# Gate rows spread by products of depth one, and a later weight low part, in a fused two-block transformer kernel

## The reference

```python
mod_x = silu(c) @ w_mod + b_mod                      # 6 vectors of 1024
sh_m, sc_m, gt_m, sh_f, sc_f, gt_f = split(mod_x, 6)
hx = modulate(rms_norm(x, g_pre_mix), sh_m, sc_m)    # h * (1 + scale) + shift
...                                                  # projections, attention, retention
x = x + gt_m * rms_norm(mix_x, g_post_mix)
hf = modulate(rms_norm(x, g_pre_ffn), sh_f, sc_f)
x = x + gt_f * rms_norm(swiglu(hf, w_ffn_in, w_ffn_out), g_post_ffn)
```

## Time and profile before

| | us |
|---|---|
| median of 3 runs (lowest, highest) | 1015.12 (1014.8, 1015.16) |
| the profiled execution, its own time | 1015.45 |
| its span in the trace | 1013.7 |
| TensorE busy | 995.3 |
| VectorE busy | 584.6 |
| ScalarE busy | 495.8 |

### The profile page before, as it was taken

One profiled execution on the slowest core, in us unless ns is written; L12 is line 12 of the kernel. 1 busy time (PEld: TensorE's weight loads), 2 busy tenths in 40 slices (PEclk: granted clock), 3 DMA queues, 4 the chain that ended last, 5 costly groups with the idle time before them and its releaser, 6 DMA issues.

```text
span 1013.7 us, 13246 instructions
## 1 busy us (share of the span) xinstructions
PE 995.3 (98%) x5164; PEld 810.6 (80%) x5164; DVE 584.6 (58%) x660; ACT 495.8 (49%) x603; POOL 0.2 (0%) x4
## 2 busy tenths in 40 slices
PE   7999999999999999999999999999999999999997
PEld 5777776778888888888888887888888878888885
DVE  5374768667555554565555665567774465555543
ACT  6473347656544443554444534663545554444432
POOL 0000000000000000000000000000000000000000
PEclk9999999999999999999999999999999999999999
DMA  9967653133655545475545465534244245555441
GB/s 373 419 272 297 274 218 126 43 121 128 213 203 173 199 169 205 166 259 174 199 166 193 166 222 182 195 125 147 102 166 166 81 147 192 198 177 202 166 166 42
DMA packets 26686, 188.32 MB, mean 186 GB/s; under 512 B 2960, under 2 KB 3216, under 8 KB 4112
## 3 DMA queue, kind: packets, MB, share of 16 engines
q1 hardware_dynamic: 26064, 185.24, 50.2%
q10 hardware_dynamic: 576, 2.43, 0.6%
HBM read 186.61 MB, written 1.05 MB: 185 GB/s over the span
## 4 chain that ended last, share of the span: by engine, by line
PE 93%; DMA 2%; DVE 2%; ACT 1%; issue 1%; SPq 1%; ACTq 0%; DVEq 0%
PE bank L1818 24%; PE bank L1820 24%; PE bank L1819 24%; DMA raw<-in_weights 2%; PE bank L2026 2%; PE bank L1862 2%; PE bank L1846 2%; PE bank L1924 2%; PE bank L1854 2%; PE bank L2292 1%; PE bank L1903 1%; PE bank L2390 1%; PE bank L2217 1%; PE bank L2168 1%; PE bank L2093 1%
## 5 line engine op out<-in xcount | busy, mean ns | idle before, releaser
L1156 DVE TENSOR_TENSOR w_lo<-raw,w_hi 128x2048 fp32r<-128x2048 f32 x148 | 338.6, 2291 | 267.6 <-ACT w_hi L641 267.4
L641 ACT ACTIVATE w_hi<-raw 128x2048 fp32r<-128x2048 f32 x148 | 283.7, 1918 | 268.1 <-PE bank L1820 217.4
L1818 PE MATMUL bank<-w_hi,hT_hi 128*128 128x512 f32 (+1 forms) x760 | 299.8, 394 | 0.0
L1820 PE MATMUL bank<-w_hi,hT_lo 128*128 128x512 f32 (+1 forms) x760 | 294.9, 388 | 0.0
L1819 PE MATMUL bank<-w_lo,hT_hi 128*128 128x512 f32 (+1 forms) x760 | 294.3, 387 | 0.0
L1818 PEld LDWEIGHTS bank<-w_hi,hT_hi 128*128 128x128 f32 x760 | 142.8, 188 | 33.0 <-issue 5.7
L1820 PEld LDWEIGHTS bank<-w_hi,hT_lo 128*128 128x128 f32 x760 | 142.7, 188 | 29.8
L1819 PEld LDWEIGHTS bank<-w_lo,hT_hi 128*128 128x128 f32 x760 | 143.0, 188 | 27.8 <-issue 0.2
L1818 PE MATMUL bank<-w_hi,gT_hi 128*128 128x512 f32 x264 | 103.4, 392 | 0.0
L1820 PE MATMUL bank<-w_hi,gT_lo 128*128 128x512 f32 x264 | 102.8, 389 | 0.0
L1819 PE MATMUL bank<-w_lo,gT_hi 128*128 128x512 f32 x264 | 102.7, 389 | 0.0
(11 more groups left out here) (310 smaller groups left out, 1008.1 us busy)
## 6 DMA issues: line engine op xcount, KB each, us to landing
raw<-in_weights SPq DMA_DIRECT2D x152, 1024.0 KB, 4.8
arena<-in_first_mods SPq DMA_DIRECT2D x8, 1024.0 KB, 14.9
memV<-in_own_mods SPq DMA_DIRECT2D x6, 1024.0 KB, 4.8
arena<-in_own_mods SPq DMA_DIRECT2D x6, 1024.0 KB, 6.9
arena<-in_const ACTq DMA_DIRECT2D x1, 1088.0 KB, 5.1
memV<-in_mem SPq DMA_DIRECT2D x1, 1024.0 KB, 6.4
x_res<-in_x SPq DMA_DIRECT2D x1, 1024.0 KB, 17.5
arena<-in_ctx SPq DMA_DIRECT2D x1, 1024.0 KB, 15.2
```

The lines of the kernel that those rows point to most:

```text
L641: act.activation(w_hi[:, v_slot, :], raw[:, u_slot, :], ACT.Copy).then_inc(hi_ready, 1)
L1156: ins = dve.tensor_tensor(w_lo[:, v_slot, n], raw[:, u_slot, n], w_hi[:, v_slot, n].bitcast(F32), ALU.subtract)
L1818: pe.matmul(out, hi, rhi, start=start, stop=False)
L1820: return pe.matmul(out, lo, rhi, start=False, stop=stop)
```

## The change

The columns of `w_mod` are laid out anew on the host, so that the third group of modulation holds the two gates and nothing else, and the first two groups hold the four scales and shifts. The gates then stay rows. Their bias and norm gains come as a new input of 128 x 1024 numbers (0.5 MB, nonzero on rows 0, 32, 64 and 96 only), loaded into `memV` by SyncE behind the load of unit `W_OUT + 1`. VectorE adds and multiplies once each on `mod_row`, and TensorE spreads each row over all partitions by a product of depth one (one row of ones, 128 columns, by one row of 512). The transposes `mod_T(2)`, `mod_columns(2)`, `gain_col` and the diagonals are gone. The four spreading products move from ahead of `mix_out(1, 0)` to behind it, and go to banks 6, 7, 0 and 2. The low part of unit `W_IN + 9` moves behind the rotations of the attention queries.

```diff
@@ banks
-    plan.signalled(("modT", 2), 7)
...
-    for q in range(4):
-        plan.signalled(("gain_row", q), 6 + q % 2)
     for q in range(2):
         plan.signalled(("mixT", q), 2 * q)
+    for q in range(4):
+        plan.signalled(("gain_row", q), [6, 7, 0, 2][q])
@@ SyncE, the loads
+                if u == RAW_AT[("w", W_OUT + 1)]:
+                    sp.wait_ge(mod_used, N_MOD)
+                    sp.dma_start(gate_rows[:, 0, :], io["gate_rows"]).then_inc(sem("gates_loaded"), 16)
@@ VectorE, after mod_columns(1)
+            chain(dve.tensor_scalar(a_ffn[:, :], mod[:, 24:32, 0], 1.0, None, ALU.add))
+            dve.tensor_tensor(a_ffn[:, :], a_ffn[:, :], col("g_pre_ffn"), ALU.mult).then_inc(sem("ffn_cols"), 1)
@@ VectorE, the query rotations
             read_out(dve, ("qa", 1))
-            low_to(W_IN + 10)
-            mod_columns(2)
-            dve.tensor_tensor(gain_col[:, 0, :], mod[:, 16:24, 0], col("g_post_mix"), ALU.mult)
-            dve.tensor_scalar(a_ffn[:, :], mod[:, 32:40, 0], 1.0, None, ALU.add)
-            chain(dve.tensor_tensor(gain_col[:, 1, :], mod[:, 40:48, 0], col("g_post_ffn"), ALU.mult))
-            dve.tensor_tensor(a_ffn[:, :], a_ffn[:, :], col("g_pre_ffn"), ALU.mult).then_inc(sem("ffn_cols"), 1)
             dve.wait_ge(sem("qa_rms"), 1)
...
                      qan[:, tb, :].rearrange("p (j k d) -> p k j d", k=KV_HEADS, d=HD), HEADS)
+            low_to(W_IN + 10)
+            read_out(dve, ("mod_row", 2))
+            dve.wait_ge(sem("gates_loaded"), 16)
+            chain(dve.tensor_tensor(mod_row[:, :], mod_row[:, :], gate_rows[:, 0, 0:512], ALU.add))
+            dve.tensor_tensor(mod_row[:, :], mod_row[:, :], gate_rows[:, 0, 512:1024], ALU.mult).then_inc(sem("gates_ready"), 1)
             low_to(W_IN + 11)
@@ VectorE, after the retention rows
-            for g in range(2):
-                gain_diagonal(g)
             split_T("mixT", n=2, first=4)
@@ TensorE, behind unit W_IN + 6
-                    if j == 6:
-                        mod_T(2)
@@ TensorE, the output projection
-            for q in range(4):
-                if q % 2 == 0:
-                    pe.wait_ge(sem(f"gain_diag{q // 2}"), 1)
-                b = free(pe, ("gain_row", q))
-                pe.matmul(b[:, :], ones, gain_diag[q // 2][:, (q % 2) * 512:(q % 2 + 1) * 512], start=True, stop=True)\
-                    .then_inc(full_sem(("gain_row", q)), 1)
             for q in range(2):
                 read_out(pe, ("mixT", q))
             mix_out(1, 0)
+            pe.wait_ge(sem("gates_ready"), 1)
+            for q in range(4):
+                b = free(pe, ("gain_row", q))
+                pe.matmul(b[:, :], ones[32 * q:32 * q + 1, :], mod_row[32 * q:32 * q + 1, :], start=True, stop=True)\
+                    .then_inc(full_sem(("gain_row", q)), 1)
             mix_out(1, 1)
```

More of the change, by code:

```diff
@@ L120 @@
 _at = 0
-for _name, _n in [("g_pre_mix", 8), ("g_post_mix", 8), ("g_pre_ffn", 8), ("g_post_ffn", 8), ("b_mod", 48),
+for _name, _n in [("g_pre_mix", 8), ("g_pre_ffn", 8), ("b_mod", 32),
                   ("ffn1_norm", 8), ("mix_norm", 8), ("xattn_norm", 8), ("mem_norm", 8), ("ffn2_norm", 8),
@@ L374, in two_blocks_kernel @@
         mod_row = sb("mod_row", [P, 512])
-        mod = sb("mod", [P, 48, 2])
+        mod = sb("mod", [P, 32, 2])
+        align = sb("align", [P, 80])
         a_mix = sb("a_mix", [P, KC, 2])
         a_ffn = sb("a_ffn", [P, KC])
-        gain_col = sb("gain_col", [P, 2, KC])
         shifted_T = sb("shifted_T", [P, 2, 2 * T])
@@ L433, in two_blocks_kernel @@
         prob_bufs = [probs, krn]
-        gain_diag = [qrn.rearrange("p a n -> p (a n)"), qan.rearrange("p a n -> p (a n)")]
+        gate_rows = memV
         rope_a, rope_b, ropes_ab = carve(at, 512), carve(at + 512, 512), carve(at, 1024); probsT = carve(at, 2, 4 * P); at += 1024
@@ L971, in _ @@
             act.wait_ge(sem("ffn_cols"), 1)
-            split_T("ffn0T", shift=(a_ffn, mod[:, 24:32, 0]))
+            split_T("ffn0T", shift=(a_ffn, mod[:, 16:24, 0]))
             split_to(W_UP[0] + 3)
@@ L1432, in normalise @@
                     dve.tensor_scalar(v, v, row_inv[:, 2 * p + kv:2 * p + kv + 1], None, ALU.mult).then_inc(sem("probs_ready"), 1)
-            def gain_diagonal(g):
-                dve.tensor_tensor(gain_diag[g].rearrange("p (k t) -> p k t", t=P), over_heads(ident, KC, P),
-                                  heads_bc(gain_col[:, g, :], KC, P), ALU.mult).then_inc(sem(f"gain_diag{g}"), 1)
             def retention_queries():
@@ L1615, in _ @@
             norm_scale(x, xn)
-            split_T("ffn0T", shift=(a_ffn, mod[:, 24:32, 0]), qs=[0, 1])
+            split_T("ffn0T", shift=(a_ffn, mod[:, 16:24, 0]), qs=[0, 1])
             low_to(W_UP[0] + 1)
-            split_T("ffn0T", shift=(a_ffn, mod[:, 24:32, 0]), qs=[2, 3])
+            split_T("ffn0T", shift=(a_ffn, mod[:, 16:24, 0]), qs=[2, 3])
             low_to(W_UP[0] + 3)
@@ L2586, in lay_out @@
     w += swiglu(f("ffn2_gate_2")[0], f("ffn2_up_2")[0], f("ffn2_down_2")[0])
-    mods = [f("w_mod")[0][k * P:(k + 1) * P, g * UNIT:(g + 1) * UNIT] for g in range(N_MOD // MOD_K) for k in range(MOD_K)]
+    parts = (0, 1, 3, 4, 2, 5)
+    w_mod = np.concatenate([f("w_mod")[0][:, D * n:D * (n + 1)] for n in parts], axis=1)
+    b_mod = np.concatenate([f("b_mod")[0][D * n:D * (n + 1)] for n in parts])
+    gates = np.zeros((P, 1024), np.float32)
+    gates[0::32, 0:512] = b_mod[4 * D:].reshape(4, 512)
+    gates[0::32, 512:] = np.concatenate([f("g_post_mix").reshape(-1), f("g_post_ffn").reshape(-1)]).reshape(4, 512)
+    mods = [w_mod[k * P:(k + 1) * P, g * UNIT:(g + 1) * UNIT] for g in range(N_MOD // MOD_K) for k in range(MOD_K)]
     units = {"w": w, "mod": mods}
@@ L2594, in lay_out @@
     small = {name: col(f(src)) for name, src in [
-        ("g_pre_mix", "g_pre_mix"), ("g_post_mix", "g_post_mix"), ("g_pre_ffn", "g_pre_ffn"),
-        ("g_post_ffn", "g_post_ffn"), ("b_mod", "b_mod"), ("ffn1_norm", "ffn1_norm_2"), ("mix_norm", "mix_norm_2"),
+        ("g_pre_mix", "g_pre_mix"), ("g_pre_ffn", "g_pre_ffn"), ("ffn1_norm", "ffn1_norm_2"), ("mix_norm", "mix_norm_2"),
         ("xattn_norm", "xattn_norm_2"), ("mem_norm", "mem_norm_2"), ("ffn2_norm", "ffn2_norm_2")]}
+    small["b_mod"] = col(b_mod[:4 * D])
     small["conv_w"] = f("conv_w_2")[0].reshape(4, P, 3).transpose(1, 0, 2).reshape(P, 12)
@@ L2607, in lay_out @@
         "first_mods": np.stack(mods[:MOD_K]), "own_mods": np.stack([mods[m] for m in OWN_MODS]),
+        "gate_rows": gates,
         "cols": np.concatenate([small[name] for name in COLS], axis=1),
```

## The result

| | before | after |
|---|---|---|
| median, executions beside each other (us) | 1014.96 (1014.76 to 1015.16) | 1030.83 (1029.75 to 1030.91) |
| profiled execution, its own time | 1015.45 | 1030.76 |
| its span | 1013.7 | 1029.2 |

The change makes the kernel slower by 15.9 us: the ratio is 1.0154 (95%: 1.0136 to 1.0171). The prediction was 1028.9, from 1023.5 to 1032.5.

What follows compares the result with a forecast made beforehand. TensorE, busy 98% of the span, was taken to bound the kernel. Late gate rows 5.8, copies ahead of a high part 5.5 and one clock fall 2.5 sum to 13.8 us: 1015.12 + 13.8 = 1028.9, range 1023.5 to 1032.5.

Steps and rivals of the forecast that it cites:

- Place one: VectorE, 142 to 177 us: gate rows land late, VectorE waits for them, and the attention loop runs 5.8 us later.
- Place two: 210 to 226 us: four copies stand ahead of a high part on ScalarE, so mix_out(1, 1) starts 5.5 us late.
- The clock at place two: TensorE's 6.2 us pause before mix_out(1, 1) drops the clock to 1.2 GHz: 2.5 us, between 0 and 3.1.
- The end of the kernel: Behind mix_out(1, 1) distances stay as now, so nothing more is lost up to the end.
- It falls at both places: Rival: the clock also falls behind the 3.3 us pause near 170 us, 2.5 us more: 1031.4 us, chance 9%.
- The clock does not fall: Rival: no clock fall behind the pause before mix_out(1, 1): 1026.4 us, chance 25%.
- No overlap: Rival: the four depth-one products come 0.8 us apart, so Place two costs 6.8 us: 1030.2 us, chance 10%.
- One wait does not end last: Rival: gate rows on chip before 150 us, Place one costs about 1.3 us: about 1024.4 us, chance 8%.
- faster: Rival: W_OUT + 3's high part is ready when the four products end and Place one vanishes: 1014.3 us, chance 3%.

Runs made afterwards that it cites:

- experiment 1: Changed kernel with the gate rows loaded one unit earlier, behind weight unit W_OUT: 1022.74 us.
- experiment 2: Changed kernel with the low part of W_IN + 9 back ahead of the reciprocals, gate-row load left where it is: 1022.57 us.
- experiment 3: Changed kernel with the gate rows issued ahead of the load of W_OUT + 1, both still behind the late low part: 1028.11 us.
- experiment 9: The kernel before, unchanged, traced a second time: 1014.49 us, last product 0.95 us sooner than in the first trace.
- experiment 4: Changed kernel with ScalarE's high part of W_OUT + 3 ahead of the four copies of the gate rows: 1026.16 us.
- experiment 5: Changed kernel with gate rows loaded behind W_OUT and the high part of W_OUT + 3 ahead of the four copies: 1019.32 us.
- experiment 7: Changed kernel with gate rows loaded behind W_OUT and the high parts of W_OUT + 3 and both value units ahead of the copies: 1014.75 us.
- experiment 11: experiment 7 with all four depth-one products taken from row 0, so three quarters of the gates are wrong: 1019.35 us.
- experiment 6: Changed kernel with ten unread products of 256 columns in TensorE's pause before mix_out(1, 1): 1028.06 us.
- experiment 8: experiment 7 with the low part of W_IN + 9 back ahead of the reciprocals: 1013.78 us.

## Why the prediction was right, and where its terms were off

**Place one: right in every step, 0.9 us short.** Gate rows on chip at 156.2 forecast, VectorE started on them at 155.78. Wait "about 6 us", 6.17. Low part of W_IN + 10 at 157.6, 157.11. TensorE's waits 0.9, 1.4 and 3.3, measured 0.94, 1.11 and 3.27. Experiments 1 and 2 show the cause: with the rows earlier, or the low part back, all that was new in them is gone. In experiment 3 they shrink with VectorE's wait. The scores of step 4 start at 176.42 instead of 170.35, 6.1 us later. The gr transposes had started 1.1 us sooner than before (149.83 against 150.91), of which 0.4 are the missing transposes and the rest had come in the first 47 us, chance by experiment 9. From there to the scores 7.1 us are lost, where the prediction had 5.8 + 0.4 = 6.2. Half of the 0.9 between them is the clock: the prediction had a fall behind the 3.3 us pause only among the rivals, at 9%. It came. From the first transposes at 171.76 to the scores of step 4 TensorE took 4.66 us, and 3.08 for the same work before. But these scores also wait for a bank that ScalarE's exponentials of step 2 set free, and ScalarE was done with those at 175.93:

```profile
175.73 0.20 ACT L836 ACTIVATION_READ_ACCUMULATOR arena<-bank,row_max 128x1 f32 x1
```

So without the fall the scores could have started 0.5 us sooner than at 176.42, and the rest of the longer products ran in a wait that was there anyway. The other 0.4 us are small differences along the chain on VectorE and ScalarE: 7.28 us from the gr transposes to the low part of W_IN + 10 (7.1 forecast), 4.17 from the first transposes of probabilities to the end of those exponentials (4.0 forecast).

**Place two: right, 0.2 us short.** `mix_out(1, 0)` waited 1.62 us for `mixT` (1.7 forecast), the four products took 1.14 us (1.1), copies, high and low part followed in this order, and TensorE stood still for 6.25 us (6.2). `mix_out(1, 1)` started at 231.27 against 219.51, 11.8 us late of which 6.1 were there already: 5.7 us, forecast 5.5. Experiments 4, 5 and 7 show that the order on ScalarE is the cause. The 1.07 us of the products is 2.8 times less than the 3.03 of full ones. The Trainium skill, "TensorE: Matmul & The Clock Gate", section "Measured speedup vs the span model", has 3.07 times for four row tiles of 512 columns, 32 rows deep; the trace agrees roughly, with 2.8 against full products and 3.4 against the serial ones of depth one (3.63, experiment 11).

**The clock at place two: right, 0.5 us short.** Fifteen products lie between 231.27 and 237.66, 6.4 us; at the 0.23 us from start to start that they have otherwise it would be 3.4. So the fall cost 3.0 us, where the prediction took 2.5 between 0 and 3.1. Experiment 6 gives nearly the same without arithmetic: 2.8 us by the medians. That it came out so near to the forecast is in part luck. Experiments 1, 2 and 3 have the same pause of 6.25 us at place two in their traces, and from the first product behind it to the next unit they take 7.81, 6.90 and 6.92 us, where the kernel after takes 8.43 and experiment 6, with the clock up, 5.58. So the fall behind one and the same pause cost 2.9 us in one trace and 2.2, 1.3 and 1.3 in others, since the clock came back sooner. The prediction had no row for that.

**The end of the kernel: the step that failed.** The prediction said that behind `mix_out(1, 1)` nothing is late, and took the end of the kernel as unchanged. The first half holds in the kernel after: the last product starts 14.4 us late, against 14.8 at 237 us. The second does not: from the start of the last product to the end of the span it is 8.6 us, 7.5 before, which is 1.1 us more. Most of this is the landing of the last store. It took 2.7 us before, and in the kernel after:

```profile
L631 SPq DMA_DIRECT2D out<-xn x1: 460/460/460, 1025.0 to 1025.0; - x1
...
DMA to landing us min/median/max: 3.6/3.6/3.6
```

The store is issued as long after the last product as before (4.39 us both times), and has the same size. In all traces with the low part behind the rotations the span ends 8.6 to 8.75 us after the last product. In the two with the low part in its old place, experiments 2 and 8, it is 7.7 and that store lands after 2.7 us, as in both traces of the kernel before. So over all fourteen traces it goes with that edit. Why a low part at 147 us should matter to a store at 1025 us stays open, and no run tells it. It is also nearly the whole difference between experiments 7 and 8, whose last products start 0.09 us apart and whose spans differ by 1.0.

**The sum.** 15.5 us of span = 7.1 + 5.7 + 3.0 + 1.1, less 0.7 of the early start, 0.4 for the transposes and 0.3 that came back later. Forecast was 13.8. The largest terms that it lacks are the 1.1 at the end and the 0.9 at place one.

**The rivals.** "It falls at both places", at 9%, is what came, and its 1031.4 is nearer to the 1030.8 measured than the forecast's 1028.9. That is in part luck, too: it priced the first fall at 2.5 us, where it cost 0.5, and had nothing for the end of the kernel. "The clock does not fall" is out by the stretches and by experiment 6, which shows the price. "No overlap" is out by the 1.14 us. "One wait does not end last" is out in the kernel after, and experiment 1 is its case: 1022.74, where the rival had 1024.4. The one on the other side, "faster", named its conditions rightly: both high part ahead of the copies and place one gone. But its price held only when the value units' high parts came ahead too. With the next one alone (experiment 5) it was 1019.3 and not 1014.3. The four copies are 2 us of ScalarE in a stretch where three high parts are due in a row, so they must be put behind the last of these, not behind the first. With that, experiment 7 has 1014.75.

## What to carry to other kernels

Before moving an instruction that frees a buffer, follow the load that waits for the buffer and every load behind it in the same queue: here the move of 2.3 us of work on an engine with slack brought half a megabyte in six us too late. An idle engine can still be the bottleneck by its order, so copies that nobody needs soon go behind all the work that TensorE needs next, not only behind the next piece. And the price of a pause of TensorE can be more than its length: behind each of those from 2.50 to 6.25 us that were new here, the clock was lower for a while.

## What the runs showed of the hardware that was not expected

- **The clock falls behind shorter pauses than the end of the kernel showed.** It fell behind 3.27, 2.90, 2.54 and 2.50 us without products, and in no trace right behind the 1.62 us for `mixT`. The price was 0.5 us behind the pause of 3.27, where other waits hid the rest, and from 1.3 to 3.0 us behind the same pause of 6.25 in four traces.
- **It can fall with no pause at all.** Behind four serial products of depth one, 3.6 us in which the profile shows TensorE busy all the time, the clock was at 0.50 in one trace and, by the mean clock, seems to have fallen in most executions of experiment 11. Behind full products of 3.0 us it did not, by the same measure, in eight executions. The Trainium skill, "TensorE: Matmul & The Clock Gate", "What's actually happening", says that the clock is set by how busy TensorE has been recently. The trace does not bear this out if busy is what the profile counts: it has TensorE busy without a gap from 220 to 225 us, and the clock at 1.00 and then at 0.50. What made it fall there stays open.
- **Depth one does not shorten a product**: 3.63 us for four on one row group, 3.03 for four full ones, 1.07 for four on four row groups.
- **The last store's landing takes 2.7 or 3.6 us**, and which of the two goes with an edit almost 900 us ahead of it. The cause is open.
